# Scaling latent-attention probabilities before their transposes, and writing the heads feature-major

## What is computed

```python
def mla_mixer(x, cos, sin, w_in, q_norm, kv_norm, w_uq, w_ukv, w_out):
    c_q, c_kv, k_rope = jnp.split(x @ w_in, [MLA_Q_RANK, MLA_Q_RANK + MLA_KV_RANK], axis=-1)
    q = (rms_norm_2(c_q, q_norm) @ w_uq).reshape(B_, S_, MLA_HEADS, MLA_NOPE + MLA_ROPE)
    kv = (rms_norm_2(c_kv, kv_norm) @ w_ukv).reshape(B_, S_, MLA_HEADS, MLA_NOPE + MLA_V)
    ...
    def attend(args):
        ...
        s = jnp.einsum('bqhd,bkhd->bhqk', qb, kf)
        s = jnp.where(key_chunk[None, :] <= q_chunk[:, None], s, -jnp.inf)
        pr = jax.nn.softmax(s, axis=-1)
        return jnp.einsum('bhqk,bkhd->bqhd', pr.astype(v.dtype), v)
    ...
    return o.astype(x.dtype) @ w_out
```

## Time and profile before

| | |
|---|---|
| median of 3 runs | 1846.87 us (1846.51 to 1847.53) |
| profiled execution | 1846.83 us, of which span 1845.0 us |
| mean granted TensorE clock | 0.999 |
| PE busy | 1827.9 us, 99% of the span |
| DVE busy | 1111.8 us, 60% |
| ACT busy | 924.1 us, 50% |
| POOL busy | 574.9 us, 31% |
| DMA | mean 177 GB/s |

### The profile page before, as it was taken

The page is one execution under the profiler, slowest core; times in us unless marked ns, Lnnn a source line. Parts: engine busy times, 40 slices in busy tenths (PEclk is TensorE's granted clock), DMA queues, the critical chain, the costliest instruction groups (busy, mean ns, idle before and its releaser), DMA issues.

```text
span 1845.0 us, 25464 instructions
## 1 busy us (share of the span) xinstructions
PE 1827.9 (99%) x10104; PEld 1579.1 (86%) x10104; DVE 1111.8 (60%) x1995; ACT 924.1 (50%) x1099; POOL 574.9 (31%) x128
## 2 busy tenths in 40 slices
PE   9999999999999999999999999999999999999998
PEld 7888888889998988888888888899888889888887
DVE  7887789886777895222867322666522287952226
ACT  7655556455554544444454444444444445454443
POOL 0000000000000007787002888300787700068870
PEclk9999999999999999999999999999999999999999
DMA  9534434644244346555433655455655543365551
GB/s 367 183 137 174 169 137 160 214 160 180 93 160 143 115 174 219 198 190 184 180 148 143 220 190 182 160 184 211 229 186 199 185 162 136 142 229 192 195 186 65
DMA packets 53193, 326.60 MB, mean 177 GB/s; under 512 B 8640, under 2 KB 11072, under 8 KB 15584
## 3 DMA queue, kind: packets, MB, share of 16 engines
q1 hardware_dynamic: 45472, 311.54, 46.3%
q10 hardware_dynamic: 7616, 13.59, 2.3%
HBM read 324.07 MB, written 1.05 MB: 176 GB/s over the span
## 4 chain that ended last, share of the span: by engine, by line
PE 93%; DVE 3%; ACT 2%; DMA 1%; issue 1%; SPq 0%; ACTq 0%; DVEq 0%
PE project L1192 37%; PE output L1192 31%; PE turn L1612 5%; PE project L1612 5%; PE project L1618 2%; PE turn L1618 2%; PE turn L1428 2%; PE output L1521 1%; PE output L1393 1%; PE output L1368 1%; PE turn L1347 1%; DMA arena<-in_ln_b 1%; PE output L1376 1%; DMA raw<-in_units 1%; DVE arena L2229 0%
## 5 line engine op out<-in xcount | busy, mean ns | idle before, releaser
L1151 POOL TENSOR_TENSOR wlo<-raw,whi 128x2048 fp32r<-128x2048 f32 x124 | 574.7, 4666 | 1221.6 <-ACT whi L1681 1204.8
L1681 ACT ACTIVATE whi<-raw 128x2048 fp32r<-128x2048 f32 x289 | 546.9, 1910 | 336.1 <-PE project L1612 166.1
L1192 PE MATMUL project<-whi,XT 128*128 128x512 f32 x1376 | 450.0, 397 | 2.3 <-DVE arena L2248 1.2
L2090 DVE TENSOR_TENSOR wlo<-raw,whi 128x2048 fp32r<-128x2048 f32 x165 | 375.1, 2286 | 21.9 <-ACT whi L1681 21.2
L1192 PEld LDWEIGHTS project<-whi,XT 128*128 128x128 f32 x1376 | 258.5, 188 | 56.3 <-issue 3.2
L1192 PE MATMUL output<-whi,YTh 128*128 128x512 f32 x736 | 288.4, 392 | 1.5 <-DVE YTl L2631 1.5
L1192 PE MATMUL output<-whi,YTl 128*128 128x512 f32 x736 | 287.1, 390 | 0.0
L1192 PE MATMUL output<-wlo,YTh 128*128 128x512 f32 x736 | 286.9, 390 | 0.0
L1192 PE MATMUL project<-wlo,XT 128*128 128x512 f32 x688 | 268.1, 390 | 0.0
L2925 DVE TENSOR_TENSOR arena<-project,arena 128x256 f32<-128x256 f32 x48 | 20.4, 425 | 408.9 <-ACT arena L2046 408.9
L1192 PE MATMUL project<-XT,whi 128*128 128x256 f32 x1184 | 219.0, 285 | 0.0
(11 more groups left out here) (292 smaller groups left out, 2311.4 us busy)
## 6 DMA issues: line engine op xcount, KB each, us to landing
raw<-in_units SPq DMA_DIRECT2D x290, 1024.0 KB, 4.8
arena<-in_ln_g ACTq DMA_DIRECT2D x8, 512.0 KB, 5.4
arena<-in_ln_b ACTq DMA_DIRECT2D x8, 512.0 KB, 6.9
xres<-in_x SPq DMA_DIRECT2D x2, 1024.0 KB, 10.5
raw<-in_units SPq DMA_DIRECT2D x2, 512.0 KB, 7.2
tok<-in_mem SPq DMA_DIRECT2D x1, 1024.0 KB, 14.3
arena<-in_x_t SPq DMA_DIRECT2D x1, 1024.0 KB, 18.1
arena<-in_mem_t ACTq DMA_DIRECT2D x1, 1024.0 KB, 4.7
```

The source lines that it names most:

```text
L1151: pool.tensor_tensor(wlo[:, slot, :], raw[:, slot, :], whi[:, slot, :], ALU.subtract).then_inc(lo_pool, 1)
L1192: mm = pe.matmul(out, x if x_stationary else w, w if x_stationary else x, start=start and i == 0, stop=stop and i == 2, skip_group_check=True)
L1681: act.activation(whi[:, slot, :], raw[:, slot, :], ACT.Copy).then_inc(hi_done, 1)
L2090: dve.tensor_tensor(wlo[:, slot, :], raw[:, slot, :], whi[:, slot, :], ALU.subtract).then_inc(lo_dve, 1)
```

## The change

Four things change, all for the heads of the latent attention alone, and one is a new cut of the output unit that all callers get.

1. **Scaling ahead of the transposes.** The free slot becomes stage N: VectorE waits for `p_ready`, takes the reciprocal of `den` and scales the two rows of blocks of `sm` in place, 128 and 256 columns, then signals `norm_ready`. TensorE's PT waits for that signal instead of `p_ready`.
2. **Values stationary.** PV becomes two products: values of key tile 0 by 256 columns of `pT`, values of key tile 1 by the last 128 columns. The result is feature-major in `PQ[3]`.
3. **No turns.** ScalarE copies `PQ[3]` to `YTh` (128 x 256, `head_hi`) and VectorE subtracts to `YTl` (`o_evac`), once for each head. `yG` is not written, and the four turns with their evacuations are gone.
4. **Output quarters between the last slots.** Quarter 0 of the first output unit stands behind the slot with PV 5 and PT 6, quarter 1 behind the slot with PV 6 and PT 7, and quarters 2 and 3 behind PV 7. The first quarter also waits for the heads 0 to 3 (`o_evac`). The step "ahead" of this unit stays behind the last slot.

```diff
@@ plan: begin_output @@
-            unit("out", (w, "Q", u, 0), ahead=not halved and ahead, hs=(0,) if halved else (0, 1), **f)
+            unit("out", (w, "Q", u, 0), ahead=not halved and ahead, xs=(0, 1) if halved else range(4), **f)
...
+        if w[0] == "mla_w_out":
+            units.append((w, "Q", 0, 0))
+            m = len(units) - 1
+
+            def piece(*xs):
+                add("out", n=m, ahead=False, xs=xs, begin=xs[0] == 0, g=g, u=0, first=True, whole=False, scan=0, src=src,
+                    conv=False, heads=len(heads), head_rows=True)
+
+            def rest():
+                add("ahead", n=m, on="sv")
+                piece(2, 3)
+
+            return g, piece, rest, lambda: (one(1), tail)[1]
+
@@ plan: output @@
+        if begun:
+            g, rest, second = begun.pop()
+            rest()
+            tail = second()
+            if before_tail is not None:
+                before_tail()
+            tail(2)
+            return g
@@ plan: quad @@
-                              stages=["T", "S", "PT", "PV"] if kind != "mla" else ["S", None, "PT", "PV"]))
+                              stages=["T", "S", "PT", "PV"] if kind != "mla" else ["S", "N", "PT", "PV"]))
@@ plan: mla @@
-        for h in range(H2):
-            slot()
-            turn("y", h, 0, "Y", 0, pre="o_evac", a=len(heads) - 4)
+        slot()
+        g, piece, rest, tail = begin_output(("mla_w_out", 0), 1024)
+        piece(0)
+        slot()
+        piece(1)
         drain()
-        late.extend(lambda h=h: turn("y", h, 1, "Y", 4, pre="o_evac", a=len(heads), late=True) for h in range(H2))
+        begun.append((g, rest, tail))
@@ TensorE: output_unit (one product of 512 columns per x; the wait per bank is as before) @@
+                for x in xs:
+                    h, c = x // 2, x % 2
+                    if first and heads_done is not None and x != 1:
+
+                        pe.wait_ge((m_ready, None, pt_evac, o_evac)[x], heads_done)
@@ TensorE: slot_stage @@
+                elif stage == "N":
+                    return
                 elif stage == "PT":
-                    pe.wait_ge(p_ready, 2 * (i + 1))
+                    if hd["kind"] == "mla":
+                        pe.wait_ge(norm_ready, j + 1)
+                    else:
+                        pe.wait_ge(p_ready, 2 * (i + 1))
...
+                    if hd["kind"] == "mla":
+                        for kt in range(2):
+                            mm = pe.matmul(PQ[3][:, kt * P:S], tok[:, kt, j * P:(j + 1) * P],
+                                           pT[:, h2, 2 * kt * P:2 * kt * P + S - kt * P], start=kt == 0, stop=kt == 1)
+                        mm.then_inc(pv_done, 1)
+                        return
@@ TensorE: step "out" @@
+                    if f["head_rows"] and f["first"]:
+                        pe.wait_ge(o_evac, f["heads"] - 4)
@@ ScalarE: step "slot" @@
+                        elif stage == "PV" and hd["kind"] == "mla":
+                            act.wait_ge(pv_done, i + 1)
+                            act.activation(YTh[:, hd["j"], :], PQ[3][:, 0:S], ACT.Copy).then_inc(head_hi, 1)
@@ VectorE: stage_of @@
+                elif stage == "N":
+                    dve.wait_ge(p_ready, 2 * (i + 1))
+                    dve.reciprocal(st[:, 88:90], den[:, kept(i), :]).then_inc(dve_own, 1)
+                    last.own()
+                    dve.wait_ge(*last.at)
+                    for h, (k0, n) in enumerate(key_spans(hd)):
+                        x = sm[:, i % 2, h * S:h * S + n]
+                        ins = dve.tensor_scalar(x, x, st[:, 88 + h:89 + h], None, ALU.mult)
+                        if h:
+                            ins.then_inc(norm_ready, 1)
...
                 elif stage == "PV":
+                    if kind == "mla":
+                        dve.wait_ge(head_hi, j + 1)
+                        dve.tensor_tensor(YTl[:, j, :], PQ[3][:, 0:S], YTh[:, j, :].bitcast(F32),
+                                                     ALU.subtract).then_inc(o_evac, 1)
...
+                        return
...
-                    y = yG[:, :, j * P:(j + 1) * P] if kind == "mla" else yA[:, :, 1024 + (j % 4) * P:1024 + (j % 4 + 1) * P]
+                    y = yA[:, :, 1024 + (j % 4) * P:1024 + (j % 4 + 1) * P]
```

33 lines of the change are left out of this document (18 added, 15 removed).

## The result

The changed kernel takes **1852.71 us** (median of 8 runs, 1851.38 to 1853.5) against 1846.89 us (8 runs) for the kernel before beside it: a ratio of 1.0029, 95% interval 1.0020 to 1.0038. It is slower by 5.8 us, where the forecast was 1.5 us faster and the range ended at 1847.6. The profiled execution took 1853.39 us, with a span of 1851.6.

A forecast was written before the change was run, and what follows sets the result against it. PE bounds the kernel; in the changed slots a VectorE-ScalarE ring of 2.55 us would bound instead. The second output unit starts at 984.19 instead of 985.70, so 1846.83 - 1.5 = 1845.3 us, range 1844.0 to 1847.6.

The forecast's parts named there:

- the relief of PE: Around the heads, cheaper PV, no turns and fewer waits free PE of at most 3.89 us.
- the sum for PE alone: If PE waited for nothing, the stretch around the heads would take 19.68 us instead of 23.57, 3.89 less.
- rival 3: Behind the heads, later work on VectorE makes PE wait and the gain is given back: 1846.8 us; chance 0.08.
- The ring: In each head slot, maximum, exponential, scaling, next maximum follow one another through VectorE and ScalarE: 2.55 us against PE's 2.29.
- Rival 1: In the head slots the scaling is hidden and PE alone bounds: -3.89 us, 1842.9 us; chance 0.05.
- hand-over: Signal between VectorE and ScalarE in the slots, taken as 0.03 us each way; 0.24 in the dearer case.
- those who could be late: Check of the 7.48 us from quarter 0 to the second output unit; PV 7 has 0.3 us to spare.
- Rival 2: On VectorE between p_ready and the next maximum, a longer turn, 2.97 us by dearer hand-over: 1847.8 us; chance 0.11.
- thin cover of subtraction and copy: On VectorE in each slot, YTl subtraction and transposes' copy, 0.98 us, fit under the 0.99 us exponential.
- Rival 4: In the head slots PE's short idle times make the clock fall to 1.2 GHz: 1862.6 us; chance 0.02.

The follow-up runs named there:

- e7: Changed kernel with the YTl subtraction one slot later, PV results in two banks in turn, and the scaling left out; 1843.56 us, ratio 0.9980.
- e2: Changed kernel with VectorE's YTl subtraction one slot later, as a fifth stage, and PV results in two banks in turn; 1845.70 us, ratio 0.9993.
- e4: Kernel before with the scaling stage alone added, PV results copied undivided, turns and output unit kept; 1849.02 us, ratio 1.0013.
- e5: Changed kernel without the output quarters, the first output unit in one piece behind the last head; 1856.91 us, ratio 1.0050.
- e6: Changed kernel with late subtraction, one more slot between scaling and transposes, three probability buffers, scaling behind the next maximum; 1845.99 us, ratio 0.9995.
- e11: Changed kernel with late subtraction placed first on VectorE, transposes' copy on ScalarE, both ScalarE copies ahead of its exponential, three probability buffers, earlier quarters; 1844.12 us, ratio 0.9979.
- the repetition of e2: The same late-subtraction, two-bank kernel as e2, run again on another chip beside the kernel before; 1846.32 us, ratio 0.9992.
- e3: Changed kernel with the copy to YTh made by VectorE, ahead of its subtraction, instead of by ScalarE; 1847.63 us, ratio 0.9996.

## Why the prediction was wrong

**What bounds the kernel, and the relief of PE: right.** PV takes 0.65 us where it doesn't wait (988.91), the sum for PE alone was out by 0.2 us (e7: -3.67 for -3.89), and behind the heads PE's waits stayed at 1.0 us, so rival 3 is out.

**The ring's own terms: right.** In e2 and e4, which hold that ring and nothing else, it takes 2.56 us for the forecast's 2.55; the scalings overlap as taken from the earlier trace rows. Rival 1 is out with it: the scaling isn't hidden as long as it stands ahead of the next maximum.

**The step that failed** is the pair of sentences behind the ring's sum: "The other two pieces of VectorE's slot, the subtraction to `YTl` (0.43) and the copy (0.55), fit under the exponential", and "ScalarE's new copy (0.38) comes ahead of the exponential ... Both cost nothing". The durations fit; the order doesn't. The copy to `YTh` is ahead of the exponential *of its own slot*, which waited for VectorE anyway, but behind that of the slot before, and that is the one VectorE's scaling waits for. So nothing fits under it: by the rows of the slot above, `YTh` until the subtraction 967.24 - 966.94 = 0.30, the subtraction 967.58 - 967.24 = 0.34 and the copy 968.05 - 967.58 = 0.47 come on top of 2.55, less the hand-over of 0.03 to the scaling, which falls away: 3.63 by this sum, 3.62 measured. What the forecast named as the thing that would break its sum, a wait of the exponential for PV, did not happen: the exponential waited for the negation (the row at 969.58). In the kernel before, VectorE divided PV's results itself and asked nothing of ScalarE there, so the earlier trace rows could show no such wait; the order of the two queues, which the change makes, did.

**The size.** From head 2's maximum on (965.08) five distances are 3.62 instead of 2.55, 5.3 us; the first is 2.56, since there is no PV yet. -1.5 + 5.3 = 3.8. The other 0.8 us of the 4.58 lie behind head 7's maximum, where the same chain holds up PV of head 6 once more:

```profile
986.28 0.92 PE L1420 MATMUL output<-arena,tok 128*128 128x256 f32 x4 [0.49 <-DVE arena L2438]
```

PE waits 0.49 us there, and the PV behind the wait takes 0.92 instead of 0.65. The forecast went through PT 7, PV 7 and quarter 3 as those who could be late, and left out PV 6, whose copy stands behind the exponential of head 7 by the same order.

**The rivals.** Rival 2 named the place (VectorE between `p_ready` and the next maximum) and the sign, and the thin cover of subtraction and copy. It was priced at 1847.8 with a chance of 0.11, since it took its price from a hand-over (0.24) and not from the work that could land in the ring if the order was another; the hand-overs measured 0.02 to 0.04 us. Its upper bound should have been all three pieces in the ring, 0.98 + 0.38 = 1.36 us a slot, and the range would then have reached 1845.3 + 6 x 1.36 = 1853.5. The durations for that bound were there, in the earlier trace rows. Rival 4 didn't happen in the slots, though they were emptier than foreseen. Busy time of the changed kernel, in the stretch of the earlier trace rows and in all slots:

```profile
973.69:979.08 5.39, 3.27 (x20) 2.34 (x18) 3.19 (x13) 2.01 (x9) 0.00 (x0) 1.00 0.00 0
...
962.00:985.00 23.00, 16.98 (x100) 13.55 (x99) 13.87 (x64) 8.19 (x34) 0.00 (x0) 1.00 0.00 0
```

With 3.27 us of work in 5.39, and 16.98 in 23.00 with seven idle times of up to 1.1 us, the granted clock stayed at 1.00. The Trainium skill's page "TensorE: Matmul & The Clock Gate" (section "A second HAM failure mode: psum-queue depth-cycling") has the clock swing when short idle times come often between groups of matmuls; in these slots it did not. It fell in e5, behind idle times of up to 2.4 us.

## What to carry to other kernels

Where a change lets two engines hand work to and fro, write down both in-order queues over two slots, with the head's number at each instruction, and follow a ring through everything that stands *ahead* of its members, not only through the members: "it ran at a time when the engine waited" is no cover if what it stands behind is what the others wait for. The bound for a cover that may fail is the covered work itself, in every slot. And once a ring is seen, moving an instruction one slot later or to the other engine is cheap: the same work, in another order, with one copy on another engine and with one more buffer of probabilities and one more result bank, was worth 7.6 us of stretch here (4.58 + 3.01).

## What the runs showed of the chip

**A fall of the clock in part of the runs.** Of the 2.0 us that the changed kernel's profile has lost ahead of the heads, 1.6 are one event at 575 us, far from the change; 0.3 are there before it (the starts 575.43 and 575.10 below) and were not traced. Busy time by stretch of the kernel before, then of the kernel after:

```profile
575.00:580.00 5.00, 4.90 (x22) 4.10 (x23) 2.88 (x2) 1.92 (x1) 0.00 (x0) 1.00 0.62 142
```

```profile
575.00:580.00 5.00, 4.57 (x13) 3.65 (x14) 2.52 (x2) 1.91 (x1) 0.00 (x0) 0.66 0.52 117
```

The same twelve products in the chain of waits, of before and of after:

```profile
575.10 2.97 PE output L1192 x12
```

```profile
575.43 4.58 PE output L1218 x12
```

Both kernels do the same there: PE stands idle for VectorE's `YTl` (1.46 us in the order of time), then starts the products. In one profile the clock stayed at 2.4 GHz, in the other it was at 1.2 GHz for some 3.5 us, and the twelve products took 1.61 us longer. Of the 12 other profiles here, those of e6, e7, e11 and the repetition of e2 show the fall (granted clock 0.66 in this stretch) and have head 1's maximum at 962.1 to 962.5; the others have 1.00 there and 960.5 to 960.9. The idle time ahead of the products is 1.46 us in all 14 profiles, with the fall and without it, so its length doesn't decide it. That the two groups of times are these two courses is a conclusion from the profiled runs. The mean clock of whole runs fits it: in e3 and e6 it is 1.000 in all eleven runs of the lower groups and 0.999 in all eleven of the upper ones. But no experiment took the idle time away, and a few runs of the kernel before (1851.8 to 1854.4 us) and one of e4_scaling_only (1854.1) lie above both groups, for a reason that no profile shows. If it is so, it explains why differences of 1 us between medians mean little here, and why the stretch, which begins behind this place, agrees better with the sums than the medians do.

**The clock and the waits of the last heads.** In the changed kernel, with its slots of 3.62 us, the quarters are worth 2 us by the waits they cover and, by the estimate above, another 4 by keeping PE busy where the clock fell without them (e5): more than the 3.9 that the relief of PE can give.
